# A backbone of linear attention and short convolutions: rows of output scales by two DMAs through DRAM in place of identity products

## The reference

```python
mod = silu_c @ ada_w[l] + ada_b[l]
sh1, sc1, g1, sh2, sc2, g2 = split(mod, 6)
h = rmsnorm(x, norm_w[l, 0]) * (1 + sc1) + sh1
y = mixer(h)                          # recurrence (l = 0) or convolution (l = 1)
x = x + g1 * rmsnorm(y, norm_w[l, 1])
hf = rmsnorm(x, norm_w[l, 2]) * (1 + sc2) + sh2
x = x + g2 * rmsnorm(swiglu(hf), norm_w[l, 3])
```

## Time and profile before

| | us |
|---|---|
| median of 3 runs | 2582.09 (2580.67 to 2584.93) |
| span of the profiled execution | 2581.9 |
| TensorE busy (matmul) | 2510.4 |
| VectorE busy | 1860.8 |
| GpSimd busy | 1299.2 |
| ScalarE busy | 1156.6 |

### The profile page before, as it was taken

One profiled execution on the slowest core, in us unless ns is written; L12 is line 12 of the kernel. 1 busy time (PEld: TensorE's weight loads), 2 busy tenths in 40 slices (PEclk: granted clock), 3 DMA queues, 4 the chain that ended last, 5 costly groups with the idle time before them and its releaser, 6 DMA issues.

```text
span 2581.9 us, 35674 instructions
## 1 busy us (share of the span) xinstructions
PE 2510.4 (97%) x12344; PEld 2094.9 (81%) x12344; DVE 1860.8 (72%) x2441; ACT 1156.6 (45%) x2159; POOL 1299.2 (50%) x859
## 2 busy tenths in 40 slices
PE   8999999999999989999999999999999999999998
PEld 6888888888887778888888877877887888888886
DVE  5377778767856476888877988888656565556898
ACT  4344534544443453333344467333454433434544
POOL 3112321431330037777877972678304767766983
PEclk8999999999999999999999999999999999999999
DMA  6123422432352343444458342032514322345533
GB/s 262 57 79 135 180 104 101 152 126 74 131 216 111 130 141 116 155 138 167 162 184 309 117 127 86 33 131 98 196 57 148 113 99 94 122 171 216 188 99 114
DMA packets 124249, 351.14 MB, mean 136 GB/s; under 512 B 12752, under 2 KB 12752, under 8 KB 121040
## 3 DMA queue, kind: packets, MB, share of 16 engines
q1 hardware_dynamic: 124112, 349.33, 38.6%
HBM read 258.58 MB, written 90.70 MB: 135 GB/s over the span
## 4 chain that ended last, share of the span: by engine, by line
PE 81%; DVE 8%; POOL 3%; issue 3%; ACT 3%; DMA 2%; SPq 1%; DVEq 0%; ACTq 0%; POOLq 0%
PE psum L1538 18%; PE psum L1540 18%; PE psum L1539 18%; PE psum L2125 4%; PE psum L2127 4%; PE psum L2126 4%; PE psum L1798 2%; PE psum L1800 2%; PE psum L1799 2%; PE psum L1750 2%; POOL row_unit_sum L1454 1%; PE psum L1737 1%; PE psum L1764 1%; PE psum L1720 1%; DVE k_all L3266 1%
## 5 line engine op out<-in xcount | busy, mean ns | idle before, releaser
L1538 PE MATMUL psum<-x_hi,unit 128*128 128x512 f32 x1232 | 483.8, 393 | 8.2 <-DVE x_lo L2967 7.7
L1540 PE MATMUL psum<-x_hi,unit 128*128 128x512 f32 x1232 | 480.2, 390 | 0.0
L1539 PE MATMUL psum<-x_lo,unit 128*128 128x512 f32 x1232 | 480.2, 390 | 0.0
L2967 DVE TENSOR_TENSOR c_set<-c_set,psum 128x512 f32<-128x512 f32 x352 | 233.1, 683 | 221.9 <-ACT c_set L2249 146.6
L1403 POOL TENSOR_TENSOR unit<-unit_sum,unit 128x512 fp32r<-128x512 f32 x200 | 291.9, 1467 | 14.1 <-ACT unit L2249 12.2
L1538 PEld LDWEIGHTS psum<-x_hi,unit 128*128 128x128 f32 x1232 | 231.8, 188 | 63.7 <-ACT c_set L2249 5.7
L1540 PEld LDWEIGHTS psum<-x_hi,unit 128*128 128x128 f32 x1232 | 231.5, 188 | 48.5
L1539 PEld LDWEIGHTS psum<-x_lo,unit 128*128 128x128 f32 x1232 | 231.8, 188 | 47.0
L1538 PE MATMUL psum<-h_hi,w_hi 128*128 128x512 f32 x624 | 262.6, 421 | 0.2 <-DVE h_lo L2967 0.2
L2125 PE MATMUL psum<-row_unit_hi,part_hi 128*128 128x512 f32 x616 | 241.9, 393 | 3.0 <-DVE part_lo L2967 1.8
L1540 PE MATMUL psum<-h_hi,w_lo 128*128 128x512 f32 x624 | 244.2, 391 | 0.0
(11 more groups left out here) (353 smaller groups left out, 5801.1 us busy)
## 6 DMA issues: line engine op xcount, KB each, us to landing
ffn_raw<-in_w_ffn_in SPq DMA_DIRECT2D x80, 512.0 KB, 5.9
part_raw<-parts_kept SPq DMA_DIRECT2D x154, 256.0 KB, 2.7
parts_kept<-part_sums SPq DMA_DIRECT2D x22, 1280.0 KB, 5.5
ada_half<-in_ada SPq DMA_DIRECT2D x96, 256.0 KB, 2.6
out_raw<-in_w_ffn_out SPq DMA_DIRECT2D x44, 512.0 KB, 7.5
w_raw<-in_w_hgrn_in SPq DMA_DIRECT2D x40, 512.0 KB, 3.6
ada_raw<-in_ada SPq DMA_DIRECT2D x32, 512.0 KB, 4.9
units_kept<-stage_unit SPq DMA_DIRECT2D x28, 512.0 KB, 2.9
```

Source lines behind the costliest of these rows:

```text
L1538: begin = pe.matmul(out_ap, hi[:, a:b], rhs_hi, start=first, stop=False)
L1539: pe.matmul(out_ap, hi[:, a:b], rhs_lo, start=False, stop=False)
L1540: return begin, pe.matmul(out_ap, lo[:, a:b], rhs_hi, start=False, stop=last)
L2967: V.tensor_tensor(dst, a, b, op).then_inc(S[sem], 1)
```

## The change

Four scales of 1024 numbers get a place in DRAM, `scale_kept`. `scale_store(sub)` writes a sub-layer's 128x8 block of `out_scale` to it, element by element, since channels that follow each other lie on different partitions. `scale_row(sub)` reads the 4 KB row back and spreads it over all 128 partitions. Both are issued by SyncE; the second waits for the completion of the first. TensorE's `out_rows` and ScalarE's `out_row_copy` are gone, and with them TensorE's waits for `row_ready`. The line numbers behind L433 shift by one, behind L918 by 14 and more.

```diff
+    scale_kept = nc.dram_tensor("scale_kept", (4, D), F32, kind="Internal").ap()
...
+            def scale_store(sub):
+                sp.wait_ge(S["mods_ready"], 2 * sub + 1)
+                sp.dma_start(scale_kept[sub].rearrange("(k p) -> p k", p=P), out_scale[:, sub * KB:(sub + 1) * KB], allow_slow_non_contiguous=True
+                             ).then_inc(S["row_stored"], 16)
+            def scale_row(sub):
+                sp.wait_ge(S["row_stored"], 16 * (sub + 1))
+                sp.wait_ge(S["x_updated"], LAT * sub)
+                sp.wait_ge(S["ada_evac"], (HEADS, G_CONV, G_CONV + CONV_GROUPS, G_CONV + CONV_GROUPS)[sub])
+                sp.dma_start(out_row[:, :], scale_kept[sub:sub + 1, :].broadcast_to([P, D])).then_inc(S["row_ready"], 16)
...
+            scale_store(0)
             sp.wait_ge(S["sigmoids"], 4 * HEADS)
             row_load(5)
             for d in (FWD, BWD):
                 sp.wait_ge(scan_sem[d], (HEADS - 1) * SCAN_STEPS + 1)
             sp.wait_ge(S["gs_ready"], HEADS)
+            scale_row(0)
             row_load(6)
...
                 pair_loads(4, 0)
+                scale_store(2 * f + 1)
...
                 pair_loads(PAIRS - 1, 1)
+                scale_row(2 * f + 1)
...
+                if p == 3:
+                    scale_store(2)
...
             for tb in range(4):
                 stream_load(1, tb)
+            scale_row(2)
...
-            def out_rows(sub, b=4):
...
-                pe.wait_ge(S["row_ready"], sub + 1)
...
-                out_rows(0, 6)
...
                     if p == 0:
-                        pe.wait_ge(S["row_ready"], sub + 1)
+                        pe.wait_ge(S["modulated"], modulated_after(block_turns(2 * f + 1, LAT - 1)[1]))
...
-                pe.wait_ge(S["modulated"], modulated_after(block_turns(2 * f + 1, LAT - 1)[1]))
-                out_rows(sub)
...
-            pe.wait_ge(S["modulated"], modulated_after(T0[3] - 1))
-            out_rows(2)
...
-            def out_row_copy(sub):
...
-                dve.wait_ge(S["row_ready"], sub + 1)
+                dve.wait_ge(S["row_ready"], 16 * sub + 16)
```

More of the change, by code:

```diff
@@ L640, in build_trunk @@
             turned modulated modulated_v h_hi_done h_ready
-            proj_full proj_evac y_scaled x_updated row_full row_ready
+            proj_full proj_evac y_scaled x_updated row_stored row_ready
             sigmoids gates_done scan_f scan_b k_merged
@@ L1636, in conv_first_panels @@
                             turn(2, turns_at[pos, kb])
-            def out_rows(sub, b=4):
-                pe.wait_ge(S["mods_ready"], 2 * sub + 1)
-                for kb in range(KB):
-                    c = sub * KB + kb
-                    mm = pe.matmul(bank(b + kb // 4, (kb % 4) * P, (kb % 4 + 1) * P),
-                                   out_scale[:, c:c + 1].broadcast_to([P, P]), ident[:, :], start=True, stop=True)
-                mm.then_inc(S["row_full"], 1)
             def ada_sums(g):
@@ L2447, in first_pair @@
                 gates_out(1)
-            def out_row_copy(sub):
-                act.wait_ge(S["row_full"], sub + 1)
-                act.wait_ge(S["x_updated"], LAT * sub)
-                b = 6 if sub == 0 else 4
-                copy(out_row[:, :], psum[:, b * HALF:(b + 2) * HALF], "row_ready")
             def stage_highs(phase, spot):
@@ L2631, in head @@
                     if hg is None:
-                        out_row_copy(0)
                         for i in (4, 5):
@@ L2688, in projection @@
                 f = sub // 2
-                if f == 1:
-                    out_row_copy(sub)
                 act.wait_ge(S["mods_ready"], 2 * inst)
```

## The result

The changed kernel takes 2599.53 us (median of 4 runs, 2597.2 to 2601.11) beside 2583.28 (4 runs, 2580.67 to 2584.93) of the kernel before on the same chip: a ratio of 1.0068, 95% interval 1.0055 to 1.0080. The forecast was 2581.2 and its range ended at 2590, so it was wrong in size and in sign.

What follows compares the result with a forecast made beforehand. TensorE, computing for 97% of the span, was taken as the bound. Terms -1.79 - 1.70 + 0 + 0 + 3.4 - 0.76 = -0.85 us on 2581.9 gave 2581.05, forecast as a median of 2581.2 us; range 2576 to 2590.

Steps and rivals of the forecast that it cites:

- Second and fourth row: Feed-forward layers: TensorE has no gap around the identity products, so removing them gains 1.79 and 1.70 us.
- ScalarE's copy at the first row: Copy stands ahead of `raw_b`, for which TensorE waits; removing it gains 0.76 us, between 0.32 and 1.03.
- The element-wise store: First row: store ahead of row 5 in the full queue delays what follows by 0.9 us, range 0 to 10.5.
- second rival: First row: store or broadcast clogs the full queue, delaying row 5 and the loads behind by 13 us; 2590.9 us, 18%.
- a store of over 3 us: First row: one of the listed observations in the trace after that would show the forecast wrong.
- Wait and broadcast: First row: queue empty 1.2 us while SyncE waits for the store, then 1.3 us for the spread row.
- Identity products in a wait: First and third row: without the products TensorE only arrives sooner at waits for loads or VectorE's sums; gain 0.
- third rival: First row: TensorE's clock also halves, after the wait for row 5 or for `mix_late`, costing 3 us; 2584.3 us, 17%.
- The broadcast for VectorE at the third row: Behind the convolutions: spread row lands at 1854.4, 3.2 us before VectorE reads it, so it is hidden.

Runs made afterwards that it cites:

- flat: Changed kernel, but each partition stores its eight values side by side (128 pieces of 32 bytes, row in another channel order): 2582.2 us, ratio 1.0007.
- first_late: Changed kernel with the first store moved behind the twelve weight loads and its broadcast behind the last weight row: 2588.3 us, ratio 1.0035.
- both: Changed kernel with the moves of first_late and conv_gap together: 2579.3 us, ratio 0.9999 against the kernel before.
- conv_gap: Changed kernel with the third store moved about 100 us earlier, to where SyncE's queue is idle: 2589.2 us, ratio 1.0038.
- row_late: Changed kernel, first store in place, but SyncE's wait for it and the broadcast moved behind the last weight row: 2598.3 us, ratio 1.0063.
- flat_c: One transfer of bench: a store of 128 pieces of 32 bytes, measured alone behind the end of the kernel before; 1.4 us.
- both_fill: Kernel of both, with the third row's eight identity products issued again on TensorE, result unread: 2579.5 us, ratio 0.9995.
- fill_two: Kernel of both_fill, with the first row's eight identity products also issued again, result unread: 2579.2 us, ratio 0.9987.
- bench: Kernel before, with eight transfers behind its end, one at a time on SyncE's otherwise idle queue; 1,024 neighbouring 4-byte pieces took 10.6 us.
- store_only: Kernel before, all identity products kept, with only the first element-wise store added and nothing waiting for it before the end: 2591.5 us, ratio 1.0041.
- bench2: Kernel before, with eleven stores behind its end, one at a time, mostly 4-byte pieces at various distances in DRAM; whole program 13,646 us.

## Why the prediction was wrong, by its own steps

**Second and fourth row: right.** -1.79 and -1.70 predicted; -1.81 to -1.83 in every trace with that edit.

**ScalarE's copy at the first row: right.** -0.76 predicted; the offset falls by 0.75 us from 810 to 879 in the changed kernel and by 0.78 in flat (0.6 in first_late and both). The row that the prediction names for it shows the products' 0.32 alone; the 0.76 stands in the same timeline, in the line of the weight load:

```profile
824.16 0.19 PEld L1798 LDWEIGHTS psum<-hgrn_row,mixed_hi 128*128 128x128 f32 x1 [0.76 <-ACT raw_b L2249]
```

**The element-wise store: mis-sized, and the main error.** 0.9 us was taken, from packets of under 512 bytes that took 13.5 ns each. In the changed kernel row 5 is 6.8 us later than it would be (788.47 in place of 783.52 - 1.87); in conv_gap, with the same code, 3.7; in row_late 7.7. Alone on the queue the store takes 10.6 us where flat_c, as many bytes, takes 1.4. The rows chosen were reads, and the step's own caveat ("they are reads, which is why the upper end stays in the range") pointed at the answer. The second rival had the right course of events (a dear store, row 5 and all behind it late, TensorE waiting) but a wrong reason, a cost of each element: the same number of elements 512 bytes apart took 2.7 us. It was given 18% and 2590.9 us, and the range ended at 2590, because only one place was thought to be exposed. The prediction had named a store of over 3 us as the sign that it was wrong, and that sign came.

**Wait and broadcast: about right.** 1.2 + 1.3 = 2.5 us predicted. From row 5 to 879 us the offset grows by 4.05 us in flat and by 1.03 in both, where no load stands behind store or broadcast: 3.0 us. The changed kernel beside row_late gives 2.9.

**Third store: a step that was not taken.** The text follows the stores of the feed-forward layers and the row that VectorE reads, and never asks what is queued behind `scale_store(2)`. It is a load that GpSimd asks for 3.3 us after its issue (landing 13.18 us after it, less the wait of 9.9). This place is 9.8 us, 8.1 of them TensorE's wait and 1.7 the half clock behind it, and conv_gap gives all of it back.

**Identity products in a wait: "gain 0" was right for the wait and wrong for the clock.** TensorE did arrive sooner and waited for the same sums (third row) and loads (first row). But 0.34 us of idle time became 2.22, and 0.88 became 2.2 even where the loads are on time (first_late, both), and behind such a pause the clock fell to half in seven of eight traces without the products at the first row, in five of seven at the third, and in none with them. The eighth is conv_gap: 2.38 us of idle time, and a granted clock of 1.00 behind it, where the fall had come 7 us sooner, behind its wait for row 6. Price, each from one pair of traces: 1.6 us at the third row (both beside both_fill), 1.8 at the first (from row 5 on, +1.03 in both and -0.77 in fill_two). The third rival named both falls of the first row, the one at row 5 (it came, at 781.9 us) and a second in the wait for `mix_late`, for which it set 3 us. It tied neither to the products that the change removes, and the third row's fall is in no rival.

The first place, worked again: 6.8 (store) + 3.0 (wait and broadcast) + 1.8 (clock) - 0.75 (copy) = 10.9, measured 11.25. The rest: 9.8 + 1.6 - 3.6 = 7.8. That the first place closes to 0.4 us is in part luck: the same sum for conv_gap, with its store at 3.7 us, gives 7.8 with the clock's fall and 6.0 without, and 6.96 was measured.

The broadcast for VectorE at the third row was hidden, as forecast: issued at 1863.78, it landed 7.8 us later, before VectorE's first use at 1876.96.

## What to carry to other kernels

- A small DMA is not a cheap DMA. Price it by what it writes: a store of 4-byte pieces from different partitions that are neighbours in DRAM made the loads behind it 4 to 9 us late here, and what counts is which load stands behind it and when that is needed. The second and fourth stores took 12 us to land and cost nothing. Put such a store where nothing is queued behind it. Runs of 32 bytes were cheap too, but no run here reads them back in the right order.
- Ask "what is behind it in this queue?" for every instance of an added DMA, not for the one place where the old code was on the critical path.
- An instruction of TensorE that lies in a wait has no price, but it may have a use: take it out, and the longer pause can cost the clock. Replaying it with an unread result brought 1.6 and 1.8 us back in the traces; the times alone don't show either.

## What the runs showed of the hardware

- **Neighbouring 4-byte writes to DRAM.** 128 from as many partitions: 6.6 and 7.1 us at a distance of 4 bytes, 2.7 at 8, 1.4 from 16 on. 1,024: 10.1 to 10.6, and 11.1 for 2,048. In bench the DMA engines show as idle meanwhile: from 2584 to 2592 us the DMA share is 0.00, with the store issued at 2581.7 and landed at 2592.3 (windows; the last three numbers are clock, share and GB/s). In the changed kernel, with row 5 queued behind the store, the share was 1.30 to 1.43 at 39 to 41 GB/s, then 0.26 to 0.50. What in the memory path makes them wait is open. The Trainium skill ("DMA: Bandwidth & Descriptors", Specifications) says that a transfer below 512 bytes is a read-modify-write. Every piece here is below that. The 128 pieces that lay 16 bytes or more apart landed in 1.4 us all the same, so size alone is not the cause.

```profile
2582.00:2584.00 2.00, 0.50 0.23 2
2584.00:2586.00 2.00, 0.50 0.00 0
```

- **Reads don't pay this.** The same 1,024 elements read singly took 2.1 us.
- **The store's hold varies.** Row 5 was late by 3.7 (conv_gap), 5.2 (store_only), 6.8 (changed) and 7.7 us (row_late) behind one and the same store.
- **A program five times as slow.** In bench2 TensorE's products of 512 columns took four times as long at a granted clock of 1.00 (before: 393 ns by the same view), from the first to the last; VectorE's sums were unchanged (685 and 683 ns). There was one execution, and the cause is open. The stores at its end took what they took in bench (6.6 and 10.1 us beside 7.1 and 10.6).

```profile
L1564 PE MATMUL psum<-x_hi,unit 128*128 128x512 f32 x1232 | 1964.6, 1595 | 0.0
```
